# The first MLP with 16 of its 22 up pairs by seven products instead of 15, in another order at the stage's two borders

## The chip, the cores and the metric

One NeuronCore of a Trainium2 chip runs the whole kernel. The metric is the device time of one execution in microseconds (us).

## The reference, cut to what matters

The kernel computes a hybrid layer (gated linear attention and sliding-window attention, then an MLP) followed by two more layers of attention and MLP, for 512 tokens of width 1024 in fp32. The change lies in the MLP of the first layer:

```python
h2 = rms_norm(x, ffn_norm)                                   # 512 x 1024
u = causal_dwconv(h2 @ w_up, conv_w, conv_b)                 # w_up: 1024 x 5632
a, bval = jnp.split(u, 2, axis=-1)                           # 2 x (512 x 2816)
return x + (jax.nn.silu(a) * bval) @ w_down                  # w_down: 2816 x 1024
```

`causal_dwconv` is a depthwise convolution over three tokens. With 128 features to a tile, `w_up` makes 22 pairs of tiles: pair i holds 128 features of `a` and the same 128 of `bval`, and gives f[i] = silu(a) * bval.

## The kernel before

Activations lie with the features on the partitions and the 512 tokens as columns. Every fp32 operand is split into a high part (fp32r, made on ACT by a copy) and a low part (the rest, by a subtraction on POOL or DVE), and each product is taken as high x high + high x low + low x high, summed in a PSUM bank.

**Plain pairs** (`up_tile`, L1217). The first N_PLAIN = 7 pairs are computed tile by tile: 8 blocks of the depth, each with 3 matmuls of 512 columns, so 24 matmuls per tile and 48 per pair. ACT makes the high part of the next weight tile (`split_hi`, L1747), POOL the low part (`split_lo`, L623). DVE scales the bank by rstd (`scaled`, L2828), ACT starts the convolution (`conv_0_of`, L2008), DVE adds its two other taps (`conv`, L2835 and L2838), ACT takes the silu (L2014), and POOL multiplies (`f_made_of`, L726).

**Product pairs** (`up_product`, L1235). The other Q_UP = 15 pairs are computed by a 2 x 2 block scheme of seven products (A11, S1, A12, S2, S4, A22, S3, in this order on PE), each of 4 blocks of depth with 3 matmuls of 256 columns: 84 matmuls of 256 columns per pair. Their left operands are blocks of the raw weights and sums of them (`up_sum` and `up_sum_low` on DVE, `up_copy` and `up_high`, L2042, on ACT, `up_low`, L720, on POOL), held in 14 slots of 512 columns. Their right operands, the seven factors, are made once from x in four parts, inside the plain pairs listed in FACTORS_AT: `factors_first` and `factors_second` on DVE (L2854 to L2865), `factor_highs` on ACT (L2020, L2021), `factor_lows` on DVE (L2871, L2874) and on POOL (L712). No product starts before all four parts have their highs and DVE's lows. The parts with odd number lie in v_tok, which is the same memory as v_split.

Results of the products are put together by ACT copies and DVE additions between them: `p1_copied` (L2047), `p5_copied` (L2054), `u2_copied` (L2060), `u3_copied` (L2066); `c_00`, `c_01`, `c_1`. PE's S2 waits for P1's copy, S4 for P5's, S3 for U2's. P1's copy of the first product pair waits on `scaled` of the last plain tile, because its counter counts all plain tiles first.

**Down projection** (L1291 on). Eight output tiles, each over the 22 f tiles; the weights come as tiles T_DOWN1, T_DOWN1 + 1, ... (T, T+1, ... below), 8 blocks each. For the first output tile (d = 0) PE takes for each weight tile the highs (L1311), then the weight's lows (L1318), and last all lows of f (L1330). f[i] gets its high part on ACT (`f_high`, L2075) and its low part on DVE (`f_low`, L2934); the weights' parts are made by `down_split_hi` (L2084) and `down_split_lo` (POOL, L737). T+2 and T+3 go into memory of the slots, T+2 being needed for f[16] to f[21].

**What sets the order.** Each engine's order is written out by hand, with semaphores between them; an engine that waits holds up all that stands behind it in its queue. SP issues the loads in one queue: raw weight pairs (`up_load`, L572) with odd number go to `stage`, the two buffers that also take all plain weight tiles; those with even number go to other memory. Before the loads of T and T+1 SP waits for

```python
sp.wait_ge(slot_low, UP_LOW_AT[HI_A22, Q_UP - 1 - (Q_UP % 2)])   # L588
```

which is POOL's last reading of the last raw pair in `stage`: pair 13 for Q_UP = 15, pair 15 for Q_UP = 16.

## Time and profile before

| | us |
|---|---|
| median of 3 runs | 1715.41 |
| lowest and highest | 1714.67, 1716.70 |
| the profiled execution's own time | 1717.3 |
| its span, first to last instruction | 1715.0 |
| PE busy | 1697.2 (99%) |
| DVE, POOL, ACT busy | 1136.6, 1027.5, 900.2 |
| mean granted TensorE clock | 0.998 |

The span leaves 2.3 us of the profiled execution's own time outside it. PE's matmuls are pipelined: one of 512 columns is shown 0.39 us long though the next starts 0.23 us after it, so idle time shown for PE is a little less than what the stream of columns loses; start to start is the better measure.

### The profile page before, as it was taken

How to read it: one execution, taken by the hardware profiler on the slowest of the kernel's cores; microseconds unless marked ns; L12 is line 12 of the kernel's file. 1: busy time of each engine (PE TensorE's matmuls, PEld its weight loads, DVE VectorE, ACT ScalarE, POOL GpSimd, SP SyncE). 2: the span in 40 equal slices, each digit the busy share in tenths (PEclk: the TensorE clock that was granted, in tenths of full speed). 3: DMA queues.
4: the chain of work that ended last, by engine and by line, in shares of the span. 5: the costliest groups of instructions: out<-in, count | busy, mean ns of one | idle time of the engine just before them, and what ended most of it. 6: DMA issues, size and time to landing. Idle time of an engine off the chain costs nothing.

```text
span 1715.0 us, 28211 instructions
## 1 busy us (share of the span) xinstructions
PE 1697.2 (99%) x9965; PEld 1458.0 (85%) x9965; DVE 1136.6 (66%) x2214; ACT 900.2 (52%) x1635; POOL 1027.5 (60%) x1076
## 2 busy tenths in 40 slices
PE   9999998999999999999999999999999999999998
PEld 7778887999788778888989898977777889898988
DVE  6875778887511455568757576767677676757576
ACT  5665545787422444435544444546565554545355
POOL 6443688777545434357666666755554665656666
PEclk9999999999999999999999999999999999999999
DMA  5211232232223222223222322232221232222222
GB/s 193 74 68 61 100 124 87 99 111 87 86 99 141 96 68 84 75 81 116 99 101 97 111 96 102 70 129 110 105 102 65 87 135 92 105 99 98 99 98 75
DMA packets 48682, 168.17 MB, mean 98 GB/s; under 512 B 5376, under 2 KB 6672, under 8 KB 48528
## 3 DMA queue, kind: packets, MB, share of 16 engines
q1 hardware_dynamic: 48272, 166.05, 27.6%
q8 instruction: 73, 1.20, 0.3%
q10 hardware_dynamic: 288, 0.52, 0.1%
q14 instruction: 49, 0.40, 0.1%
HBM read 164.31 MB, written 2.24 MB: 97 GB/s over the span
## 4 chain that ended last, share of the span: by engine, by line
PE 80%; DVE 12%; ACT 4%; issue 2%; POOL 1%; DMA 1%; SPq 0%; DVEq 0%; ACTq 0%; POOLq 0%
PE bank L926 18%; PE bank L1685 6%; PE bank L1694 6%; PE bank L1686 6%; PE bank L850 4%; PE bank L851 4%; PE bank L856 4%; PE bank L944 3%; PE bank L950 3%; PE bank L945 3%; PE bank L1266 3%; DVE arena L3438 3%; PE bank L1274 3%; PE bank L1267 3%; PE bank L1318 2%
## 5 line engine op out<-in xcount | busy, mean ns | idle before, releaser
L623 POOL TENSOR_TENSOR w_lo<-stage,w_hi 128x256 fp32r<-128x256 f32 x664 | 532.7, 835 | 421.4 <-ACT w_hi L1747 217.9
L1747 ACT ACTIVATE w_hi<-stage 128x1024 fp32r<-128x1024 f32 x166 | 174.7, 1053 | 156.0 <-PE bank L926 51.7
L851 PE MATMUL bank<-xn_lo,w_hi 128*128 128x512 f32 x544 | 211.7, 389 | 0.0
L850 PE MATMUL bank<-xn_hi,w_hi 128*128 128x512 f32 x544 | 211.7, 389 | 0.0
L926 PE MATMUL bank<-xn_hi,w_hi 128*128 128x512 f32 x464 | 189.0, 407 | 0.0
L926 PE MATMUL bank<-xn_lo,w_hi 128*128 128x512 f32 x464 | 181.8, 392 | 0.0
L3418 DVE TENSOR_TENSOR x<-x,bank 128x256 f32<-128x256 f32 (+1 forms) x217 | 97.5, 455 | 89.2 <-PE bank L1694 86.5
L1694 PE MATMUL bank<-arena 128*128 128x256 f32 x896 | 146.6, 283 | 0.0
L856 PE MATMUL bank<-xn_hi,w_lo 128*128 128x512 f32 x544 | 135.0, 389 | 0.0
L1685 PE MATMUL bank<-arena 128*128 128x256 f32 x512 | 129.4, 284 | 1.3 <-DVE arena L3438 0.6
L1686 PE MATMUL bank<-arena 128*128 128x256 f32 x512 | 128.7, 283 | 0.0
L1694 PEld LDWEIGHTS bank<-arena 128*128 128x128 f32 x896 | 124.8, 192 | 0.0
L926 PE MATMUL bank<-xn_hi,w_lo 128*128 128x512 f32 x464 | 123.9, 398 | 0.0
L856 PEld LDWEIGHTS bank<-xn_hi,w_lo 128*128 128x128 f32 x544 | 102.1, 188 | 21.2
L851 PEld LDWEIGHTS bank<-xn_lo,w_hi 128*128 128x128 f32 x544 | 102.1, 188 | 21.1
L850 PEld LDWEIGHTS bank<-xn_hi,w_hi 128*128 128x128 f32 x544 | 102.2, 188 | 20.9
L3438 DVE TENSOR_TENSOR arena<-tmp,arena 128x256 fp32r<-128x256 f32 (+2 forms) x128 | 115.5, 921 | 3.8 <-ACT arena L2453 2.5
L926 PEld LDWEIGHTS bank<-xn_hi,w_hi 128*128 128x128 f32 x464 | 87.2, 188 | 25.1 <-issue 8.5
L926 PEld LDWEIGHTS bank<-xn_hi,w_lo 128*128 128x128 f32 x464 | 84.6, 188 | 22.8 <-issue 6.0
L926 PEld LDWEIGHTS bank<-xn_lo,w_hi 128*128 128x128 f32 x464 | 87.3, 188 | 16.0
L1685 PEld LDWEIGHTS bank<-arena 128*128 128x128 f32 x512 | 98.2, 192 | 2.8 <-issue 2.7
L1686 PEld LDWEIGHTS bank<-arena 128*128 128x128 f32 x512 | 98.2, 192 | 0.0
(511 smaller groups left out, 4308.9 us busy)
## 6 DMA issues: line engine op xcount, KB each, us to landing
stage<-weights SPq DMA_DIRECT2D x189, 512.0 KB, 3.2
stage<-pairs SPq DMA_DIRECT2D x46, 512.0 KB, 3.2
prob<-pairs SPq DMA_DIRECT2D x32, 512.0 KB, 3.3
bias<-table SPq DMA_DIRECT2D x11, 896.0 KB, 5.5
xn_raw<-pairs SPq DMA_DIRECT2D x14, 512.0 KB, 4.1
out<-y SPq DMA_DIRECT2D x8, 256.0 KB, 2.2
x<-x_in SPq DMA_DIRECT2D x3, 512.0 KB, 7.3
bias<-swa_table SPq DMA_DIRECT2D x4, 256.0 KB, 3.6
```

The source lines that it names most:

```text
L623: ins = nc.gpsimd.tensor_tensor(w_lo[:, p_, ks], stage[:, p_, ks], w_hi[:, p_, ks].bitcast(F32), ALU.subtract)
L850: pe.matmul(G[p_][:], w_hi[:, p_, k], hi[:, k], start=(first and k == ks[0]), stop=False)
L851: mm = pe.matmul(G[p_][:], w_hi[:, p_, k], lo[:, k], start=False, stop=False)
L856: mm = pe.matmul(G[p_][:], w_lo[:, p_, k], hi[:, k], start=False, stop=(last and k == ks[-1]))
L926: mm = pe.matmul(G[p_][:], (w_hi if i < 2 * KD else w_lo)[:, p_, k], (xn_lo if i < 2 * KD and i % 2 else xn_hi)[:, k], start=(i == 0), sto ...
L944: pe.matmul(G[dd][:], w, ff_hi[:, k], start=(k == k0), stop=False)
L1685: pe.matmul(region, w, fc_hi[:, i, f], start=(fresh and i == 0), stop=False, skip_group_check=True)
L1686: pe.matmul(region, w, fc_lo[:, i, f], start=False, stop=False, skip_group_check=True)
L1694: mm = pe.matmul(region, w, fc_hi[:, i, f], start=False, stop=(i == QUADS - 1), skip_group_check=True)
L1747: act.activation(w_hi[:, p_], stage[:, p_], ACT.Copy).then_inc(hi_ready, 1)
L3418: dve.tensor_tensor(dst, dst, src, ALU.add).then_inc(product_added, 1)
L3438: dve.tensor_tensor(fc_lo[:, i, a:b + 1].rearrange("p c s -> p (c s)"), src, fc_hi[:, i, a:b + 1].rearrange("p c s -> p (c s)").bitcast(F3 ...
```

## The change

N_PLAIN goes from 7 to 6, so one pair moves from the plain way to the seven products and Q_UP becomes 16. FACTORS_AT stays at pairs 0, 1, 3, 4, of which 4 is now the last of the loop. The first slots to be filled (A11, S1, A12, S2) move from v_split and bias_slots to bias_slots and rstd_slot, and S4 and S3 to v_split, so that ACT's wait for all factor lows stands ahead of S4's high instead of A11's. The down projection's T+2 and T+3 swap their places, and T+3's high now waits for the last product. In the plain loop ACT makes the factor highs ahead of the next weight's highs; DVE makes the factor lows ahead of the convolution's taps and the second half of the factors ahead of the second convolution. At the end of the products ACT takes f[11] and f[12] ahead of the last U3 copy, f[13] ahead of the last convolution's start, and all of f[16] to f[21] ahead of T+3's high; DVE does `c_1` of the last pair ahead of f_low of f[9].

```diff
--- before.py
+++ after.py
@@ -48,7 +48,7 @@
 
 N_IN = 18
 N_OUT = KD
-N_PLAIN = 7
+N_PLAIN = 6
 FACTORS_AT = [0, 1, 3, 4]
 Q_UP = NF1 - N_PLAIN
 N_UP1 = 2 * N_PLAIN
@@ -223,8 +223,8 @@
         flat_bias = bias[:].rearrange("p a b c -> p (a b c)")
         factor = arena[:, N_IN_ARENA:2 * NF1].rearrange("p (c a r) s -> p c a (r s)", c=7, a=2)
         factor_parts = [arena_raw[:, 6:10].rearrange("p k s -> p (k s)"), v_tok[:].rearrange("p a b t f -> p (a b t f)")]
-        up_slots = ([v_split[:, a, b].rearrange("p t f -> p (t f)") for a in range(2) for b in range(2)] +
-                    [bias_slots[:, k] for k in range(7)] + [rstd_slot[:]])
+        up_slots = [bias_slots[:, k] for k in range(7)] + [rstd_slot[:]]
+        up_slots += [v_split[:, a, b].rearrange("p t f -> p (t f)") for a in range(2) for b in range(2)]
         up_slots += [xn_hi[:, 0], xn_hi[:, 1]]
         up_hi = {k: up_slots[2 * i] for i, k in enumerate(SLOT_ORDER)}
         up_lo = {k: up_slots[2 * i + 1] for i, k in enumerate(SLOT_ORDER)}
@@ -251,18 +251,18 @@
 
         def down_hi(t):
 
+            if t == T_DOWN1 + 3:
+                return v_split[:, 0].rearrange("p b t f -> p (b t) f")
             if t == T_DOWN1 + 2:
-                return v_split[:, 0].rearrange("p b t f -> p (b t) f")
-            if t == T_DOWN1 + 3:
                 return bias_slots[:, 0:2].rearrange("p a (c f) -> p (a c) f", f=P)
             a = N_IN_ARENA + 4 * F_FREE[t % 2]
             return arena[:, a:a + 2].rearrange("p a (c f) -> p (a c) f", f=P)
 
         def down_lo(t):
 
+            if t == T_DOWN1 + 3:
+                return v_split[:, 1].rearrange("p b t f -> p (b t) f")
             if t == T_DOWN1 + 2:
-                return v_split[:, 1].rearrange("p b t f -> p (b t) f")
-            if t == T_DOWN1 + 3:
                 return bias_slots[:, 2:4].rearrange("p a (c f) -> p (a c) f", f=P)
             a = N_IN_ARENA + 4 * F_FREE[t % 2] + 2
             return arena[:, a:a + 2].rearrange("p a (c f) -> p (a c) f", f=P)
@@ -2078,7 +2078,7 @@
 
                 act.wait_ge(stage_full[t % 2], 16 * (t // 2 + 1))
                 if t < T_DOWN1 + 4:
-                    act.wait_ge(product_done, N_PROD * (Q_UP - 1) + (1, 2, UP_AT[HI_S1], UP_AT[HI_S2])[t - T_DOWN1])
+                    act.wait_ge(product_done, N_PROD * (Q_UP - 1) + (1, 2, UP_AT[HI_S1], UP_AT[HI_S3])[t - T_DOWN1])
                 else:
                     act.wait_ge(hi_free, t - 1)
                 act.activation(down_hi(t), stage[:, t % 2], ACT.Copy).then_inc(hi_ready, 1)
@@ -2092,17 +2092,17 @@
                     up_copy(0)
                 silu(i)
                 conv_0_of(i, 1)
+                if i in FACTORS_AT:
+                    factor_highs(FACTORS_AT.index(i))
                 if i < N_PLAIN - 2:
                     split_hi(T_MLP1 // 2 + i + 2, 0)
-                if i in FACTORS_AT:
-                    factor_highs(FACTORS_AT.index(i))
-            act.wait_ge(ff_ready, FF_PREP)
-            act.wait_ge(factor_low, QUADS)
             up_high(HI_A11, 0)
             up_high(HI_S1, 0)
             up_high(HI_A12, 0)
             conv_0_of(N_PLAIN - 1, 0)
             up_high(HI_S2, 0)
+            act.wait_ge(ff_ready, FF_PREP)
+            act.wait_ge(factor_low, QUADS)
             up_high(HI_S4, 0)
             up_copy(1)
             for q in range(Q_UP):
@@ -2140,20 +2140,21 @@
                 conv_0_of(i, 0)
                 if more:
                     up_high(HI_A22, q + 1)
+                else:
+                    f_high(11)
+                    f_high(12)
                 if q + 2 < Q_UP:
                     up_copy(q + 2)
             u3_copied(Q_UP - 1)
-            f_high(11)
-            f_high(12)
+            f_high(13)
             conv_0_of(NF1 - 1, 1)
             silu(NF1 - 1)
-            for f in range(13, 16):
-                f_high(f)
+            f_high(14)
+            f_high(15)
             down_split_hi(T_DOWN1 + 2)
-            for f in range(16, NF1 - 1):
+            for f in range(16, NF1):
                 f_high(f)
             down_split_hi(T_DOWN1 + 3)
-            f_high(NF1 - 1)
             load_exp_and_ln()
             n_split = 4
             for d in range(KD):
@@ -2935,16 +2936,16 @@
 
             for i in range(N_PLAIN - 1):
                 scaled(i, 0)
-                conv(i, 0)
                 if i - 1 in FACTORS_AT:
                     factor_lows(FACTORS_AT.index(i - 1))
+                conv(i, 0)
                 if i in FACTORS_AT:
                     factors_first(FACTORS_AT.index(i))
                 scaled(i, 1)
+                if i in FACTORS_AT:
+                    factors_second(FACTORS_AT.index(i))
                 if i < N_PLAIN - 2:
                     conv(i, 1)
-                if i in FACTORS_AT:
-                    factors_second(FACTORS_AT.index(i))
             if N_PLAIN - 2 in FACTORS_AT:
                 factor_lows(FACTORS_AT.index(N_PLAIN - 2))
             for k in (HI_S1, HI_S3, HI_S2, HI_S4):
@@ -2978,8 +2979,8 @@
                 elif EARLY_AT <= q < EARLY_AT + N_EARLY:
                     f_low(q - EARLY_AT)
                 conv(i, 0)
+            c_1(Q_UP - 1)
             f_low(N_EARLY + 1)
-            c_1(Q_UP - 1)
             f_low(N_EARLY + 2)
             conv(NF1 - 1, 1)
             for f in DVE_LOWS:
```

## Rows read from the trace of the kernel before

**Rows 1.** The page, part 1: busy time, share of the span, instructions.

```profile
PE 1697.2 (99%) x9965; PEld 1458.0 (85%) x9965; DVE 1136.6 (66%) x2214; ACT 900.2 (52%) x1635; POOL 1027.5 (60%) x1076
```

**Rows 2.** PE, timeline, plain pairs: start us, length us, line, shape, count, [idle <-releaser].

```profile
210.27 0.39 PE L1226 MATMUL bank<-xn_hi,w_hi 128*128 128x512 f32 x1
...
221.15 0.39 PE L1226 MATMUL bank<-xn_hi,w_hi 128*128 128x512 f32 x1
...
275.61 2.11 PE L1231 MATMUL bank<-xn_hi,w_lo 128*128 128x512 f32 x8 [0.95 <-POOL w_lo L623]
```

**Rows 3.** PE, timeline, product pairs.

```profile
277.56 0.28 PE L1266 MATMUL bank<-arena,v_split 128*128 128x256 f32 x1
...
282.74 0.35 PE L1266 MATMUL bank<-arena,bias_slots 128*128 128x256 f32 x1 [0.71 <-ACT rstd L2047]
...
285.75 0.36 PE L1266 MATMUL bank<-arena,bias_slots 128*128 128x256 f32 x1 [1.35 <-ACT bank L2054]
...
412.50 0.28 PE L1266 MATMUL bank<-arena,v_split 128*128 128x256 f32 x1
```

**Rows 4.** PE, timeline, first tile of the down projection.

```profile
432.66 0.63 PE L1311 MATMUL bank<-w_hi,arena 128*128 128x512 f32 x2
...
442.83 0.50 PE L1311 MATMUL bank<-arena,v_split 128*128 128x512 f32 x1 [0.97 <-ACT arena L2075]
443.63 2.70 PE L1318 MATMUL bank<-arena,v_split 128*128 128x512 f32 x6 [0.30 <-POOL v_split L737]
...
451.73 0.39 PE L1311 MATMUL bank<-w_hi,v_split 128*128 128x512 f32 x1
```

**Rows 5.** Windows, tail: stretch, its length, busy by engine, PEclk, DMA share, GB/s.

```profile
444.00:446.00 2.00, 2.00 (x6) 1.61 (x5) 2.00 (x5) 0.08 (x1) 0.00 (x0) 0.50 0.58 201
```

**Rows 6.** DVE, timeline, last plain pairs.

```profile
255.41 0.75 DVE L2835 SCALAR_TENSOR_TENSOR tmp<-bank,par,tmp 128x511 f32<-128x511 f32 x1 [1.92 <-ACT tmp L2008]
...
256.87 1.24 DVE L2871 TENSOR_TENSOR arena<-arena_raw,arena 128x256 fp32r<-128x256 f32 x1
...
259.17 1.23 DVE L2854 SCALAR_TENSOR_TENSOR v_tok<-x,par,rstd 128x512 f32<-128x512 f32 x1
...
262.79 0.70 DVE L2828 TENSOR_TENSOR bank<-bank,rstd 128x512 f32<-128x512 f32 x1
...
265.79 0.56 DVE L2864 TENSOR_TENSOR v_tok<-v_tok 128x256 f32<-128x256 f32 x1
...
267.14 0.69 DVE L2828 TENSOR_TENSOR bank<-bank,rstd 128x512 f32<-128x512 f32 x1
...
273.50 0.69 DVE L2828 TENSOR_TENSOR bank<-bank,rstd 128x512 f32<-128x512 f32 x1
...
281.43 0.69 DVE L2828 TENSOR_TENSOR bank<-bank,rstd 128x512 f32<-128x512 f32 x1
```

**Rows 7.** ACT, timeline: last factor highs; last product pair.

```profile
267.58 1.47 ACT L2021 ACTIVATE arena<-v_tok 128x1536 fp32r<-128x1536 f32 x1
...
425.16 1.06 ACT L2084 ACTIVATE arena<-stage 128x1024 fp32r<-128x1024 f32 x1
...
427.20 1.05 ACT L2084 ACTIVATE arena<-stage 128x1024 fp32r<-128x1024 f32 x1
...
429.71 0.37 ACT L2060 ACTIVATE rstd<-bank 128x256 f32<-128x256 f32 x1
```

**Rows 8.** POOL, timeline, around the end of the products.

```profile
426.29 2.84 POOL L737 TENSOR_TENSOR arena<-stage,arena 128x256 fp32r<-128x256 f32 x4 [0.72 <-ACT arena L2084]
...
437.39 1.61 POOL L726 TENSOR_TENSOR xn_raw<-tmp 128x512 f32<-128x512 f32 x1 [3.75 <-DVE tmp L2838]
438.96 4.62 POOL L737 TENSOR_TENSOR v_split<-stage,v_split 128x256 fp32r<-128x256 f32 x4
```

**Rows 9.** SP, timeline of the DMA issues; issue to landing for the first two loads.

```profile
413.60 44.81 SPq L489 DMA_DIRECT2D stage<-weights  x7
...
DMA to landing us min/median/max: 3.2/3.7/4.1
```

## The prediction

> **What bounds the kernel.** The page comes first: PE is busy 99% of the span [rows 1], so a change can only shorten PE's stream or close its gaps. All PE times below are start to start. The second view is PE's timeline through the stage. A plain pair takes 221.15 - 210.27 = 10.88 us, a tile 5.44 [rows 2]. The tiles from 210.27 on are 12, ideally 65.28 us, and the first product starts at 277.56 [rows 3]: 2.0 us are lost, in the last pair, where PE waits for weights (0.95 for POOL's low part) [rows 2]. The two product pairs between 412.50 [rows 3] and 432.66 [rows 4] take 20.16, so 10.08 each. Fifteen of them would take 151.2; from 277.56 to 432.66 are 155.1, so 3.9 us are lost, 2.4 of them at the start of the first pair: S2 starts at 282.74 where 277.56 + 3 x 1.44 = 281.88 was due, and S4 at 285.75 where 284.18 was [rows 3]. The first tile of the down projection has 66 matmuls of 512 columns, 66 x 0.227 = 15.0 us, and takes 432.66 to 451.73, 19.1 [rows 4]: 4.1 lost. In it the matmul of f[21] starts at 442.83 behind ACT's f_high, about 1.7 after its due time of 441.1; the lows of T+2 start at 443.63 behind POOL, another 0.6; and the 28 matmuls from 443.63 take 8.10 in place of 6.35, 1.75 more. The third view says why: the granted clock is 0.50 in 444 to 446 [rows 5], the lower level (1.2 GHz), after some 2 us with hardly a matmul. So the stage loses 10 us at its borders, and the change touches all of them; its arithmetic is small.
>
> **The change, part by part** (times in the clock of the old trace).
>
> *The pair itself.* One plain pair goes, one product pair comes: 10.08 - 10.88 = **-0.80** on PE. The other engines have steady slack beside a product pair: PE is busy without a gap there already.
>
> *The end of the plain pairs.* PE needs 10 tiles from 210.27, so the last ends at 264.67, and A11 may start at 264.8. Before, four parts of factors were done two pairs ahead of the end; now the last is made in the last loop round. On the old timing this would be ruin: DVE starts scaling the second tile of pair 4 at 262.79, 9 us after PE finished it (253.8), and has finished the factors only at 267.14 [rows 6]. But DVE had idled, 1.92 us at a time, for ACT's start of the convolution [rows 6], and the new order puts factor work into these waits. I worked DVE's queue through from pair 0: it catches up with PE in pair 2 and starts pair 4 when its first tile is done, 210.27 + 7 x 5.44 = 248.4. From there: scaling 0.6, lows of part 2 2.30 (256.87 to 259.17), taps 1.46 (255.41 to 256.87), first factors 3.62 (259.17 to 262.79), scaling 0.6, second factors 1.35 (265.79 to 267.14) [rows 6]: 258.4. ACT's highs end 1.9 later (269.05 [rows 7] against 267.14), at 260.3, DVE's last lows 1.15 later, at 261.4. That is 3.4 ahead of A11's start. POOL's lows of the last weight tile no longer stand behind the factor lows, so the 2.0 of stalls go. Products start 264.8 in place of 277.56, with a pair less: 277.56 - 10.88 - 264.8 = **-1.9**.
>
> *The first products.* They stay DVE-bound. From the end of the factor lows (274.10, 0.6 after 273.50) to the scaling of the last tile DVE has 7.33 of work (to 281.43), and S2 starts 1.31 after that [rows 3, 6]. The queue there is unchanged: 261.4 + 7.33 + 1.31 = 270.0 against 264.8 + 4.32 = 269.1 due: a stall of 0.9, as before (0.86). ACT's queue from P1's to P5's copy is unchanged, so S4's 1.57 stays. New slots take only a wait away from ACT that is over by then: 0. The chain from 248.4 to 261.4 is put together from durations taken with POOL at work beside DVE, as it will be; a twelfth of it either way, my estimate, is 1 us, and would be passed on to S2 in full. So **+0.1**, between -0.5 (S2's stall can't be less than none) and +1.0.
>
> *The loads of T and T+1.* Nothing in the diff's lines shows this: Q_UP is now even, the last raw pair (15) lies in `stage`, and SP's wait at L588 is for it. The old loads go out at 413.60, 1.10 after pair 13's start [rows 3, 9]; the new ones the same 1.10 after pair 15's, 423.7 where pair 15's start stands for the old 412.50 + 10.08 = 422.6. The first lands 3.2 later, the second, issued 0.5 after it, 4.1 later [rows 9]: 426.9 and 428.3. ACT took T's high at 425.16 and T+1's at 427.20 [rows 7]; now it stands there with P5's and U2's copies behind it. P5's copy follows T's high (0.95) and ends at 428.3; S4 is due at 432.66 - 3 x 1.44 = 428.34. T+1's high starts at 428.35, so the U2 copy, 2.51 after it (427.20 to 429.71 [rows 7]), at 430.9; S3 is due at 431.2 and the copy takes 0.4. PE loses **+0.15**. Bounds: if the first load lands as late as the second, 4.1, all this is 0.9 later, +1.1; if the wait were hidden, 0.
>
> *The first down tile.* f[21]'s high moves ahead of T+3's (1 us): ACT is done with it at about 441.2, in time; the 1.7 in front of 442.83 goes. What is late next: POOL's lows of T+2, which stand behind f[21]'s product on POOL (437.39) and so behind DVE's last taps [rows 8]. DVE has these one f_low sooner by the new order, but the U2 copy and with it C_01, the taps of (21, 0) and C_1 come 1.1 later by ACT's wait; then f_low of f[9] and f[10]. I get POOL free for the lows at 439.3, in place of 438.96. They took 4.62, though the same four operations took 2.84 at 426.29 [rows 8]. In the first case DVE was at its f_lows; it will be again, so I take 4.62: lows of T+2 from 444.0 in place of 443.63. So the f[21] stall is merely swapped for a longer wait on POOL, **+0.4**, with the 28 matmuls at the lower clock as before. The Trainium skill (GPSIMD Engine Reference, Key points) says that GpSimd shares its SBUF interfaces with VectorE and contends with VectorE instructions that have two SBUF inputs, as an f_low has; by that rule 4.62 holds again, while 2.84 would take 1.8 more off. Rows 8 agree with it.
>
> T+3's lows wait on the 20th f low and are due only 5 us into the second down tile: 0. Later stages see the same tiles in the same buffers: 0.
>
> **Sum**: -0.80 - 1.9 + 0.1 + 0.15 + 0.4 = -2.05. The profiled execution has a span of 1715.0 and 2.3 around it; -2.05 gives 1712.95 and 1715.25. Its own 1717.3 stands 1.9 over the median of the runs, 1715.41, which gives 1713.4. A measurement of this kernel tells 0.2% (3.4 us) from no change, so this is "no change".
>
> **Rivals.**
> 1. *The clock stays up in the tail.* The stretch without a matmul will be 2.7 us in one piece in place of two shorter ones around f[21]'s matmul. For a fall speaks that it is longer; against it, that it is solid and lies elsewhere. If the clock holds, 1.75 more is saved: 1711.6. The Trainium skill (TensorE: Matmul & The Clock Gate, The HAM clock gate) says that the monitor runs freely and the point of a change varies from run to run; by that rule equal gaps need not have equal clocks, and no row here decides. Chance 0.2.
> 2. *The tail closes:* POOL's lows at 2.84: 1.8 less, then also no lower clock: -5.6, 1709.8. Against it [rows 8]. Chance 0.05.
> 3. *The clock falls at the first products* too: 2.4 us idle between 281.88 and 285.75 [rows 3] were followed by products at full speed before, but the place moves by 13 us. Costs up to 1.75: 1715.1. Chance 0.15.
> 4. *Slower: DVE doesn't catch up.* S2 waits on DVE's chain at once, us for us, since the slack of 3.4 lies in A11 only. If DVE reaches the end of the last factors at 267.1 as before and not at 258.4, S2 comes 8.7 later: 1713.4 + 8.7 = 1722.1. It decides against the change from 2.1 us of lateness on, measurably from 5.5. For it: DVE was 9 us behind PE. Against it: its idle time before taps, which the order fills. Chance 0.1.
>
> Forecast 0.5. Faster by over 0.2%: rivals 1 and 2, 0.24 (and a little of them falls short); slower: most of rival 4 with a late load, 0.09; the rest 0.67. **Range**: 1710.5 (rival 1 and the low bounds) to 1716.6 (rival 3, first factors and load at their high bounds); rival 2, rival 4 are left out.
>
> **What would show it.** Right: no wait of PE in the last plain pair, A11 at 264.8 with all factor lows done by 262, S2 at about 270.1 behind P1's copy; ACT's high of T waiting for a DMA, 1.8 later against PE than before; f[21] without a stall, one wait on POOL ahead of T+2's lows, ending 11.4 after PE's first down matmul (before 11.0), and granted clock 0.50 behind it. Wrong: A11 or S1 waiting for factor lows (rival 4), a P5 or U2 stall over 1 us in the last pair (load later), a full clock in the tail (rival 1).

## The result, and the profile after

The changed kernel takes 1718.45 us (median of 20 runs, 1715.54 to 1720.44) against 1716.47 for the kernel before (20 runs): ratio 1.0014, 95% interval 1.0008 to 1.0020. It is slower by 2.0 us, where 2.05 us less was forecast. The profiled execution took 1718.22 us with a span of 1716.4, 1.4 more than before. The first line is page part 1 of the changed kernel, to be held against [rows 1].

```profile
PE 1694.8 (99%) x10001; PEld 1459.0 (85%) x10001; DVE 1140.0 (66%) x2222; ACT 903.8 (53%) x1645; POOL 1025.5 (60%) x1073
```

PE is busy for 2.4 us less and the span is 1.4 longer, so PE waits more. The timeline of PE in the changed kernel shows where: the first product, the waits in the first two pairs and the last one, and the first tile of the down projection.

```profile
264.58 0.28 PE L1266 MATMUL bank<-arena,bias_slots 128*128 128x256 f32 x1
...
267.18 0.75 PE L1274 MATMUL bank<-arena,bias_slots 128*128 128x256 f32 x4 [1.48 <-POOL bias_slots L720]
...
272.18 0.36 PE L1266 MATMUL bank<-arena,bias_slots 128*128 128x256 f32 x1 [1.39 <-ACT rstd L2047]
...
275.20 0.35 PE L1266 MATMUL bank<-arena,v_split 128*128 128x256 f32 x1 [1.35 <-ACT bank L2054]
...
286.18 0.36 PE L1266 MATMUL bank<-arena,v_split 128*128 128x256 f32 x1 [0.64 <-ACT bank L2054]
...
421.60 0.28 PE L1266 MATMUL bank<-arena,bias_slots 128*128 128x256 f32 x1
...
429.11 0.36 PE L1266 MATMUL bank<-arena,v_split 128*128 128x256 f32 x1 [1.59 <-ACT bank L2054]
...
433.50 0.63 PE L1311 MATMUL bank<-w_hi,arena 128*128 128x512 f32 x2
...
445.06 2.48 PE L1318 MATMUL bank<-arena,bias_slots 128*128 128x512 f32 x6 [2.55 <-POOL bias_slots L737]
...
453.11 0.39 PE L1311 MATMUL bank<-w_hi,bias_slots 128*128 128x512 f32 x1
```

Start to start, with [rows 2 to 4] beside it:

| term | predicted | measured | from |
|---|---|---|---|
| the pair itself | -0.80 | -0.80 | 10.08 - 10.88 |
| end of the plain pairs | -1.9 | -2.1 | 264.58 - (277.56 - 10.88); 0.1 of it lies before the stage |
| first products | +0.1 | +2.0 | below |
| late load of T, T+1 | +0.15 | +1.75 | S4 at 429.11; due 421.60 + 4 x 1.44 = 427.36 |
| first down tile | +0.4 | +0.54 | (453.11 - 433.50) - (451.73 - 432.66) |
| sum | -2.05 | +1.4 | span 1716.4 - 1715.0 |

421.60 is the start of the last pair's A11. All products take 433.50 - 264.58 = 168.92 where 16 x 10.08 = 161.28 were due, 7.64 lost; 1.75 of them stand before S4 of the last pair and 5.9 at the start. Before it was 3.9, all at the start. Of the 2.0 more, S4 of the first pair shows 2.4: it comes 10.62 behind A11 (275.20 - 264.58), before 8.19 (285.75 - 277.56 [rows 3]); 0.4 is won back in the second pair.

In the stretches of the trace around the tail's wait (the columns as in [rows 5]) the granted clock is at its lower level (1.2 GHz) behind the gap, as before:

```profile
444.00:446.00 2.00, 0.94 (x3) 0.82 (x4) 2.00 (x3) 0.21 (x1) 1.00 (x1) 0.90 0.00 0
446.00:448.00 2.00, 2.00 (x6) 1.58 (x5) 2.00 (x5) 0.00 (x0) 0.57 (x1) 0.50 0.79 256
```

**The first border.** DVE's timeline in the changed kernel, from the last plain tiles to the last factor lows:

```profile
248.47 0.70 DVE L2829 TENSOR_TENSOR bank<-bank,rstd 128x512 f32<-128x512 f32 x1
249.07 0.42 DVE L2872 TENSOR_TENSOR arena<-arena_raw,arena 128x256 fp32r<-128x256 f32 x1
249.41 0.69 DVE L2875 TENSOR_TENSOR arena<-arena_raw,arena 128x512 fp32r<-128x512 f32 x1
250.74 0.75 DVE L2836 SCALAR_TENSOR_TENSOR tmp<-bank,par,tmp 128x511 f32<-128x511 f32 x1 [0.65 <-ACT tmp L2008]
...
252.19 1.30 DVE L2855 SCALAR_TENSOR_TENSOR v_tok<-x,par,rstd 128x512 f32<-128x512 f32 x1
253.42 1.78 DVE L2857 SCALAR_TENSOR_TENSOR v_tok<-x,par,rstd 128x512 f32<-128x512 f32 x1
255.23 2.50 DVE L2859 TENSOR_TENSOR v_tok<-v_tok 128x256 f32<-128x256 f32 x1
257.66 0.96 DVE L2860 TENSOR_TENSOR v_tok<-v_tok 128x256 f32<-128x256 f32 x1
258.65 0.70 DVE L2829 TENSOR_TENSOR bank<-bank,rstd 128x512 f32<-128x512 f32 x1
...
262.94 0.69 DVE L2875 TENSOR_TENSOR arena<-v_tok,arena 128x512 fp32r<-128x512 f32 x1 [0.95 <-ACT arena L2021]
```

and POOL's in the same time:

```profile
252.91 1.74 POOL L726 TENSOR_TENSOR arena_raw<-tmp 128x512 f32<-128x512 f32 x1
254.61 2.84 POOL L712 TENSOR_TENSOR arena<-arena_raw,arena 128x1024 fp32r<-128x1024 f32 x1
257.42 3.37 POOL L623 TENSOR_TENSOR w_lo<-stage,w_hi 128x256 fp32r<-128x256 f32 x4
262.98 2.91 POOL L712 TENSOR_TENSOR arena<-v_tok,arena 128x1024 fp32r<-128x1024 f32 x1 [2.20 <-ACT arena L2021]
265.85 2.52 POOL L720 TENSOR_TENSOR bias_slots<-arena_raw,bias_slots 128x512 fp32r<-128x512 f32 x2
```

DVE starts pair 4 at 248.47, as worked out (248.4). But its four first factors then take 258.65 - 252.19 = 6.46 us and not 3.62. An operation of 256 columns takes 2.50: it starts in POOL's one instruction of 1024 columns and ends 0.28 behind it (257.73, 257.45). In the kernel before the same four stood beside `split_lo` (L623), in four short instructions.

The other terms of DVE's chain moved too. The lows of part 2 take 1.0 us where the sum had 2.30: in [rows 6] POOL was at work beside them, here it is idle. DVE then waits 0.65 for ACT's start of the convolution, the second factors take 0.4 more than worked out, and the last lows end 0.6 behind ACT's highs and not 1.15. Together that is 2.84 + 0.65 + 0.4 - 1.3 - 0.5 = 2.1. So the last lows end at 263.55 (262.94 and the 0.6 of a step), 2.15 behind the forecast 261.4, and S2 starts at 272.18, 2.18 behind the forecast 270.0. Besides, POOL's factor lows of the last part start when the highs end (262.98) and hold up A11's lows behind them (265.85): the first wait of PE, 1.48, which the prediction did not have. It costs nothing of its own, since S2 waits for DVE's chain anyway.

**The load.** SP's timeline of the issues, then ACT's in the last pair; [rows 9] and [rows 7] answer to them:

```profile
422.69 9.40 SPq L489 DMA_DIRECT2D stage<-weights  x3
```

```profile
427.64 1.06 ACT L2084 ACTIVATE arena<-stage 128x1024 fp32r<-128x1024 f32 x1 [3.34 <-DMA stage<-weights]
428.60 0.37 ACT L2054 ACTIVATE bank<-bank 128x256 f32<-128x256 f32 x1
```

SP issues T's load at 422.69, 1.09 behind the last pair's start (forecast 1.10), and it lands 4.9 later, not 3.2. P5's copy, and with it S4, stands behind ACT's wait.

### The profile page after: what moved, and what is told of

Its sections match the earlier page's. It is cut to its first block, busy times and chain, and to the rows that moved or that the text cites. A ratio compares the mean times of both kernels' runs of the same rounds, so it can differ in the third digit from the quotient of the medians.

```text
span 1716.4 us, 28306 instructions
## 1 busy us (share of the span) xinstructions
PE 1694.8 (99%) x10001; PEld 1459.0 (85%) x10001; DVE 1140.0 (66%) x2222; ACT 903.8 (53%) x1645; POOL 1025.5 (60%) x1073
## 4 chain that ended last, share of the span: by engine, by line
PE 87%; DVE 6%; ACT 2%; issue 2%; POOL 2%; DMA 1%; SPq 0%; DVEq 0%; ACTq 0%; POOLq 0%
PE bank L926 18%; PE bank L1685 6%; PE bank L1694 6%; PE bank L1686 6%; PE bank L851 6%; PE bank L850 6%; PE bank L856 6%; PE bank L944 3%; PE bank L950 3%; PE bank L945 3%; PE bank L1266 2%; PE bank L1274 2%; PE bank L1267 2%; PE bank L1318 2%; PE bank L1311 2%; PE bank L1313 2%
## 5 line engine op out<-in xcount | busy, mean ns | idle before, releaser
L623 POOL TENSOR_TENSOR w_lo<-stage,w_hi 128x256 fp32r<-128x256 f32 x656 | 522.5, 830 | 418.5 <-ACT w_hi L1747 219.3
```

What stands on the lines that cost most here:

```text
L623: ins = nc.gpsimd.tensor_tensor(w_lo[:, p_, ks], stage[:, p_, ks], w_hi[:, p_, ks].bitcast(F32), ALU.subtract)
```

## The experiments

Three groups, each with its own runs of the kernel before. All differences are from the changed kernel unless it says otherwise. For each run the table gives, from PE's timeline of its profile: the start of the first product (A11); what the products lose (start of the first down matmul, less A11, less 10.08 per product pair); the idle time of PE before the last pair's S4, or S3 in pair_only, of that; and the first down tile, start to start. Then the span of that execution and the ratio to before of all runs.

| kernel | pairs plain | A11 | products lose | of it last pair | down tile | span | ratio, 95% |
|---|---|---|---|---|---|---|---|
| before | 7 | 277.56 | 3.9 | 0 | 19.07 | 1715.0 | 1 |
| after | 6 | 264.58 | 7.6 | 1.59 | 19.61 | 1716.4 | 1.0014 (1.0008-1.0020) |
| after_again | 6 | 264.80 | 9.8 | 1.71 | 19.48 | 1718.4 | 1.0022 (1.0013-1.0031) |
| pair_only | 6 | 269.58 | 5.8 | 0.94 | 19.45 | 1719.4 | 1.0024 (1.0015-1.0033) |
| orders_only | 7 | 277.27 | 2.1 | 0 | 16.91 | 1710.8 | 0.9978 (0.9968-0.9988) |
| early_load | 6 | 265.42 | 6.9 | 0 | 16.92 | 1714.5 | 1.0000 (0.9991-1.0009) |
| split_lows | 6 | 264.49 | 7.0 | 0.36 | 18.03 | 1714.1 | 1.0006 (0.9997-1.0016) |
| factors_early | 6 | 270.21 | 5.5 | 1.40 | 18.03 | 1718.4 | 1.0020 (1.0011-1.0029) |
| tail_swap | 6 | 264.80 | 6.9 | 0.33 | 15.44 | 1711.9 | 1.0000 (0.9990-1.0009) |
| all_three | 6 | 269.98 | 2.5 | 0 | 14.99 | 1712.2 | 0.9992 (0.9983-1.0001) |
| pool_order | 6 | 264.85 | 9.2 | 1.72 | 19.63 | 1718.2 | 1.0012 (1.0003-1.0021) |
| best_six | 6 | 264.59 | 7.2 | 0 | 14.99 | 1711.6 | 0.9993 (0.9984-1.0002) |
| seven_tail | 7 | 275.97 | 2.2 | 0 | 14.99 | 1707.6 | 0.9965 (0.9953-0.9977) |

### pair_only: the pair without the orders

```diff
--- before.py
-N_PLAIN = 7
+N_PLAIN = 6
```

> The kernel before with N_PLAIN = 6 and nothing else. Theory A (the new order is what lets DVE finish the factors in time): DVE finishes the last factors several us late, the first products wait for them, S2 comes 5 to 9 us late; the late load of T adds 1 to 2 us; 7 to 10 us slower than before. Rival B (the order in the plain loop hardly matters, the moved pair brings all the cost itself): within 1 us of the changed kernel, so about 1.5 to 2.5 us slower than before.

Measured: 1720.36 us, ratio 1.0024. PE's timeline, the first product:

```profile
269.58 0.58 PE L1266 MATMUL bank<-arena,v_split 128*128 128x256 f32 x1 [4.97 <-ACT v_split L2042]
```

and DVE's, the same four operations as above:

```profile
258.95 1.23 DVE L2854 SCALAR_TENSOR_TENSOR v_tok<-x,par,rstd 128x512 f32<-128x512 f32 x1
...
261.35 0.84 DVE L2858 TENSOR_TENSOR v_tok<-v_tok 128x256 f32<-128x256 f32 x1
262.12 0.41 DVE L2859 TENSOR_TENSOR v_tok<-v_tok 128x256 f32<-128x256 f32 x1
262.57 0.70 DVE L2828 TENSOR_TENSOR bank<-bank,rstd 128x512 f32<-128x512 f32 x1
```

With the old order they take 3.62 us (262.57 - 258.95), but come 6.8 later. So the new order brings DVE forward, and it is this shift against POOL's queue that makes them 6.46. A11 waits 4.97 for the factors and the slots, and the whole is 4.1 us slower than before by the ratio, 5.0 between the medians. That lies between the two expectations (7 to 10, and 1.5 to 2.5): A11 is late as theory A has it, but the products then lose 1.8 less than in the changed kernel (5.8 against 7.6).

### orders_only: the orders without the pair

```diff
-N_PLAIN = 6
+N_PLAIN = 7
```

> The changed kernel with N_PLAIN = 7 again: all the reordering and the moved slots, but 15 product pairs, so the last raw pair is not in stage and L588 waits for pair 13. Theory A: no DMA wait on ACT at T's high, no stall of the last S4, no weight stall in the last plain pair, the down projection's first tile about as long as before (18 to 19.6 us); 1 to 4 us faster than before. Rival B (the orders themselves cost the time): slower than before by about what the change is, 2 us.

Measured: 1711.88 us, 0.9978: a clear gain of 3.8 us (0.0022 x 1715.4). In the table, against before, it is -0.3 for A11, -1.8 in the products and -2.2 in the down tile. Against the changed kernel's span (1716.4 against 1710.8) the pair therefore costs 5.6, and the table gives its parts: -0.8 for the pair, -1.8 for A11 (264.58 against 277.27 - 10.88), +5.5 lost in the products (1.75 of it at the load) and +2.7 in the down tile. The last was not in the prediction: with seven plain pairs the wait for T+2's lows is short and the clock stays up behind it. PE's timeline of orders_only:

```profile
440.99 1.67 PE L1318 MATMUL bank<-arena,bias_slots 128*128 128x512 f32 x6 [1.59 <-POOL bias_slots L737]
...
447.51 0.39 PE L1311 MATMUL bank<-w_hi,bias_slots 128*128 128x512 f32 x1
```

The six lows take 1.67 in place of 2.48, and from there to the next tile are 6.52 in place of 8.05.

One row of DVE in this profile warns against taking short POOL instructions for harmless:

```profile
240.50 4.36 DVE L2855 SCALAR_TENSOR_TENSOR arena_raw<-x,par,rstd 128x512 f32<-128x512 f32 x1
```

It has two inputs in SBUF, and POOL is at work beside it without a pause until 244.31, in instructions of 256 columns (`split_lo`) and one `f_made`. It ends 0.55 behind the last of them. In the changed kernel the same operation beside the same work took 0.99; in early_load it took 4.23 and in split_lows 3.16.

### early_load: the load of T and T+1 off its late place

```diff
-            sp.wait_ge(slot_low, UP_LOW_AT[HI_A22, Q_UP - 1 - (Q_UP % 2)])
-            loads(T_DOWN1, T_QKV[0])
+            sp.wait_ge(slot_low, UP_LOW_AT[HI_A22, Q_UP - 2])
+            for r in range(2):
+                sp.dma_start(down_raw(T_DOWN1 + r), weights[T_DOWN1 + r]).then_inc(stage_full[r], 16)
+            loads(T_DOWN1 + 2, T_QKV[0])
```

`down_raw` is free memory of the raw pairs (xn_raw 8 to 11), which ACT and POOL then read in place of `stage`.

> The changed kernel, with the raw tiles T and T+1 loaded into xn_raw blocks 8 to 11 as soon as pair 14 is read, instead of stage after pair 15. Theory A (the load behind pair 15 is a cost of its own): the last S4's stall of 1.75 us goes, and ACT, DVE and POOL reach the tail earlier, so that the lows of T+2 start 10 to 10.5 us after PE's first down matmul instead of 11.6; 2 to 4 us faster than the changed kernel. Rival B (DVE's chain sets the tail anyway): S4's stall goes and the same time is lost again in the tail, 0 to 0.5 us faster.

Measured: 1716.28 us, 1.0000. ACT's timeline shows T's high without a wait, and PE has no wait in the last pair; the wait in the tail (PE's row) is 1.59 as in orders_only:

```profile
426.12 1.06 ACT L2092 ACTIVATE arena<-xn_raw 128x1024 fp32r<-128x1024 f32 x1
```

```profile
444.01 1.67 PE L1326 MATMUL bank<-arena,bias_slots 128*128 128x512 f32 x6 [1.59 <-POOL bias_slots L745]
```

So the late load costs twice: the stall before S4, and, through POOL, whose lows of T and T+1 come late, 1 us more gap in the tail, behind which the clock fell. In the table that is 1.59 and 2.7 us; of the 2.7, 1.6 is the clock, since split_lows has the long gap (2.55) with the clock up and takes 18.03. Only part of it shows in the span (1.9 less). A11 came 0.8 later in this run, its first border lost 1.0 more (with the operation of 4.23 us DVE ends the last lows 1.6 later), and behind the down tile it took 0.7 longer. By the ratios the gain is 2.4 us, the low end of theory A.

### split_lows: POOL's long instruction cut in four

```diff
-                nc.gpsimd.tensor_tensor(factor[:, F_T1:, 1, ks], factor_parts[k % 2][:, 2 * S:].rearrange("p (c s) -> p c s", c=4),
-                                        factor[:, F_T1:, 0, ks].bitcast(F32), ALU.subtract).then_inc(factor_low, 1)
+                for c in range(4):
+                    ins = nc.gpsimd.tensor_tensor(factor[:, F_T1 + c, 1, ks], factor_parts[k % 2][:, 2 * S + c * HS:2 * S + (c + 1) * HS],
+                                                  factor[:, F_T1 + c, 0, ks].bitcast(F32), ALU.subtract)
+                ins.then_inc(factor_low, 1)
```

> The changed kernel, with POOL's factor lows as four instructions of 256 columns instead of one of 1024. Theory A (a DVE operation with two SBUF inputs is held up for as long as one POOL instruction, so a long one holds it long): DVE's 256-column L2859 beside it falls from 2.50 us to about 1, the first factors from 6.46 to 4 to 4.5, and all behind them comes about 2 us earlier: A11's lows without a stall, S2 1.5 to 2 us earlier, kernel 1.5 to 2 us faster than the changed kernel. Rival B (what is shared is the bandwidth, whatever the length): first factors 6 us or more, no change beyond 0.3 us.

Measured: 1717.39 us, 1.0006. DVE's timeline, then POOL's:

```profile
252.97 1.30 DVE L2857 SCALAR_TENSOR_TENSOR v_tok<-x,par,rstd 128x512 f32<-128x512 f32 x1
254.20 1.77 DVE L2859 SCALAR_TENSOR_TENSOR v_tok<-x,par,rstd 128x512 f32<-128x512 f32 x1
256.01 0.85 DVE L2861 TENSOR_TENSOR v_tok<-v_tok 128x256 f32<-128x256 f32 x1
...
257.77 0.70 DVE L2831 TENSOR_TENSOR bank<-bank,rstd 128x512 f32<-128x512 f32 x1
```

```profile
255.39 3.63 POOL L713 TENSOR_TENSOR arena<-arena_raw,arena 128x256 fp32r<-128x256 f32 x4
```

The one DVE operation falls from 2.50 to 0.85 and the four from 6.46 to 4.80, though POOL's work has become longer (3.63, not 2.84). It is the length of POOL's instruction that DVE was held for. What is left of the excess is 1.77 for 1.22, beside `f_made` (1.74 long). S2 comes only 0.7 earlier (271.50), since the operation of 3.16 us had made DVE 0.8 late at the first factors. The landing of T's load happened to be a quick one here (3.7), and PE lost 0.36 in the last pair. The gain over the changed kernel, 1.1 us between the medians, can't be told from nothing: the intervals of the two ratios overlap. So the cause of DVE's 2.50 is shown in the trace, and not by the time of the whole kernel.

### after_again: the changed kernel once more, beside the next three

> The changed kernel once more, in the same chip job as the next three. Theory A (the load of T behind pair 15 lands at times that differ from execution to execution, and PE waits for all of it above about 3.3 us): time as measured, about 0.1 to 0.2% over before; in this profile the load's time to landing and the last S4's stall move together (stall = landing - 3.2, within 0.3 us), and both differ from the first profile's 4.9 and 1.75. Rival B (4.9 is what this load always takes here, something beside it slows it): landing 4.8 to 5.0 again.

Measured: 1720.17 us, 1.0022. Here the clock fell at the first products as well (rival 3). The windows of this run:

```profile
268.00:272.00 4.00, 3.90 (x24) 3.90 (x25) 3.93 (x7) 1.67 (x3) 3.56 (x4) 0.71 0.00 0
272.00:276.00 4.00, 2.81 (x18) 2.43 (x17) 2.78 (x5) 3.98 (x8) 1.99 (x3) 0.87 0.01 2
```

S4 stands 8.07 behind A11's lows (276.17 - 268.10), as in the first profile (275.20 - 267.18 = 8.02): the slow matmuls lie in what S2's wait would have been. pool_order and best_six show the same: S4 is 8.05 behind A11's lows in both, with the clock up in the one and fallen in the other. The products lose 2.2 us more than in the first profile (9.8 against 7.6). 0.75 of it is in the first pair, and begins with a plain weight tile whose load ACT waited for, 1.14 us where the first profile has 0.27:

```profile
249.94 1.06 ACT L1747 ACTIVATE w_hi<-stage 128x1024 fp32r<-128x1024 f32 x1 [1.14 <-DMA stage<-weights]
```

ACT's start of the convolution stands behind it, so DVE begins its first factors 0.96 later (253.15), and S4 comes 0.97 later. Another 1.3 is in the second pair (S4 to S4 12.29, and 10.98 in the first profile). The lower clock is not needed for that: split_lows shows 12.19 there at the full clock.

T's load landed 5.0 us after its issue, as rival B has it. But split_lows and tail_swap, with the same load, show 3.7, so 4.9 is not what it always takes; and landing less 3.2 gives PE's stall within 0.2 us each time, as theory A has it.

### factors_early: the last part of the factors one pair sooner

```diff
-FACTORS_AT = [0, 1, 3, 4]
+FACTORS_AT = [0, 1, 2, 3]
```

> The changed kernel with FACTORS_AT = [0, 1, 2, 3]: the last factors a pair sooner. Theory A (the first products are late because the last factors are made in the last round, with DVE's first factors stretched to 6.5 us by POOL's work): A11's lows without a stall, S2's stall 0.3 to 1 us in place of 1.55, 2.5 to 3.5 us faster than the changed kernel. Rival B (the first products are bound by the sums and the scaling of the last tile, whatever the factors do): A11's stall goes, but S2 and S4 come as late after the last tile as before: 0 to 1.5 us faster.

Measured: 1719.36 us, 1.0020, no gain. PE's timeline has new waits in the plain pairs:

```profile
242.09 2.10 PE L1231 MATMUL bank<-xn_hi,w_lo 128*128 128x512 f32 x8 [0.73 <-POOL w_lo L623]
...
255.87 2.11 PE L1231 MATMUL bank<-xn_hi,w_lo 128*128 128x512 f32 x8 [1.36 <-POOL w_lo L623]
...
258.92 0.50 PE L1226 MATMUL bank<-xn_hi,w_hi 128*128 128x512 f32 x1 [0.94 <-ACT w_hi L1747]
```

A11's lows and S2 no longer wait, and the products lose 4.3 us less than in after_again (5.5 against 9.8). But A11 starts at 270.21, 5.4 later. Four parts in four pairs in a row are more than ACT and POOL can do beside the weights; the same work, due earlier, takes its price before the border.

### tail_swap: T+2's parts ahead of the last product of f

```diff
@@ POOL
             down_split_lo(T_DOWN1 + 1)
-            f_made_of(NF1 - 1)
             down_split_lo(T_DOWN1 + 2)
+            f_made_of(NF1 - 1)
@@ ACT
             f_high(13)
+            down_split_hi(T_DOWN1 + 2)
             conv_0_of(NF1 - 1, 1)
             silu(NF1 - 1)
             f_high(14)
             f_high(15)
-            down_split_hi(T_DOWN1 + 2)
```

> The changed kernel with T+2's high on ACT ahead of the last convolution's start, and its lows on POOL ahead of f[21]'s product. Theory A (the tail's wait is POOL's queue: f[21]'s product and then lows slowed by DVE): the wait ahead of T+2's lows falls from 2.55 to under 0.5 us, the granted clock stays at its upper level behind it; PE's first down tile takes 15 to 16.5 us in place of 19.6; 3 to 4.5 us faster than the changed kernel. Rival B (f[21]'s high becomes late instead, since its product now stands behind the lows): the wait moves to the last L1311, 1 us or more, 0.5 to 2 us faster.

Measured: 1715.82 us, 1.0000, 4.35 less than after_again in the same group. POOL's timeline:

```profile
435.65 3.63 POOL L737 TENSOR_TENSOR bias_slots<-stage,bias_slots 128x256 fp32r<-128x256 f32 x4
439.23 1.74 POOL L726 TENSOR_TENSOR xn_raw<-tmp 128x512 f32<-128x512 f32 x1
```

The lows are done before PE wants them. In this tile PE waits 0.15 for f[21]'s high and nowhere else, the clock is 1.00 in all windows from 440 to 446, and the tile takes 15.44 us, of which 15.0 is arithmetic.

### all_three: early_load, factors_early and tail_swap

> Early load of T and T+1, factors a pair sooner and the swap in the tail together on the changed kernel. Theory A (three separate places, so the gains add): 7 to 10 us faster than the changed kernel, 1708 to 1711 us, faster than the kernel before by 0.3 to 0.5%. Rival B (one gives back what another saves): 3 to 6 us faster than the changed kernel.

Measured: 1714.67 us, 0.9992. The tail has no wait left (14.99) and the products lose only 2.5, but the waits in the plain pairs are those of factors_early and take it back: A11 at 269.98. At 5.5 us less than after_again it is within rival B's 3 to 6: theory A had added up gains that two of the parts don't have together.

### pool_order: POOL's long instruction moved instead of cut

```diff
                 split_lo(T_MLP1 // 2 + i + 1, 0)
+                if i == 4:
+                    split_lo(T_MLP1 // 2 + i + 1, 1)
                 if i:
                     f_made_of(i - 1)
                 if i - 1 in FACTORS_AT:
                     factor_lows(FACTORS_AT.index(i - 1))
-                split_lo(T_MLP1 // 2 + i + 1, 1)
+                if i != 4:
+                    split_lo(T_MLP1 // 2 + i + 1, 1)
```

> The changed kernel, with POOL's order in the last round of the plain loop changed: both lows of the last weight pair first, then f[3]'s product and the third factor lows, so that DVE's first factors run beside L623 and no longer beside L726 and L712. Theory A (the failing term is DVE's first factors, 6.46 us beside L726 and the long L712 against 3.62 beside L623): L2855 to L2860 take 3.6 to 4.2 us, the last lows end 2 to 2.8 us sooner, A11's lows have no stall or under 0.5 us, S2's stall is near 1 us; 2.5 to 4 us faster than the changed kernel. Rival B (L623 slows DVE as much, its rows of before were lucky): first factors 5.5 us or more, under 1 us faster.

Measured: 1717.55 us, 1.0012, as the changed kernel. DVE's timeline, then POOL's:

```profile
253.17 1.30 DVE L2858 SCALAR_TENSOR_TENSOR v_tok<-x,par,rstd 128x512 f32<-128x512 f32 x1
...
257.42 0.70 DVE L2832 TENSOR_TENSOR bank<-bank,rstd 128x512 f32<-128x512 f32 x1
258.02 1.50 DVE L2868 TENSOR_TENSOR v_tok<-v_tok 128x256 f32<-128x256 f32 x1
259.55 2.50 DVE L2869 TENSOR_TENSOR v_tok<-v_tok 128x256 f32<-128x256 f32 x1
```

```profile
257.95 1.29 POOL L726 TENSOR_TENSOR arena_raw<-tmp 128x512 f32<-128x512 f32 x1
259.20 2.57 POOL L712 TENSOR_TENSOR arena<-arena_raw,arena 128x1024 fp32r<-128x1024 f32 x1
```

The first factors fall to 4.25 (257.42 - 253.17), as they should if what POOL does beside them makes them slow. But now the second factors lie beside POOL's two long instructions, the first 1.50 and the second again 2.50, where they took 0.93 and 0.85. Each ends 0.28 behind the POOL instruction that it started in (259.52 and 259.24, 262.05 and 261.77). The cause is confirmed a second time, and the gain is nil: the contention has been moved along DVE's chain, not taken out. The last lows even end 1.0 later than in the changed kernel (264.51), because ACT waited 1.00 us for a plain weight tile's load and DVE began its first factors that much later (253.17).

### best_six: pool_order, early_load and tail_swap

> The changed kernel with POOL's new order, the early load of T and T+1 and the swap in the tail. Theory A (three separate places): 7 to 10 us faster than the changed kernel, 1709 to 1712 us, spans within 1 us of each other in nearly all runs, since no load and no fall of the clock is left that differs. Rival B (one gives back what another saves, as with the factors a pair sooner): 1713 us or more.

Measured: 1714.12 us, 0.9993. The load and the tail cost nothing any more (14.99); the first border still loses 7.2, and the clock fell in it (granted 0.62 from 268 to 272). The contention that pool_order only moves is still there, so the border's share of what was expected did not come, and the time is rival B's (1713 us or more).

### seven_tail: seven plain pairs, the new orders and tail_swap

> The changed kernel with N_PLAIN = 7 and the swap in the tail: 15 product pairs, all orders new. Theory A: the tail's wait of 1.59 us goes; 1 to 2 us faster than orders_only, near 1710 us, and 0 to 2 us faster or slower than best_six, since the pair itself is worth only 0.8 us. Rival B (the tail is already closed enough): within 0.5 us of orders_only.

Measured: 1709.6 us (6 runs, 1708.24 to 1711.37), 0.9965 (0.9953 to 0.9977). It beats both kernels, the one before by about 6 us. PE does not wait in the last plain pairs, the products lose 2.2 and the tail nothing. Against tail_swap the only difference is the pair: it costs 4.3 us by the spans (1711.9 against 1707.6) and about 6 by the ratios (1.0000 against 0.9965).

## Why the prediction was wrong

**The pair, -0.80:** right, as a term of PE's stream. What the runs add is that the pair is worth no more than that, and that with it the kernel is 4 to 7.5 us slower in every comparison (pair_only 4.1 over before, after and after_again 6.2 and 7.5 over orders_only, tail_swap 6 over seven_tail, by the ratios): it has to have its factors a pair sooner, and its number being odd or even decides when T is loaded.

**The end of the plain pairs, -1.9:** right. A11 at 264.58 (forecast 264.8), no wait in the last plain pair, DVE at pair 4 at 248.47 (248.4). Rival 4 (DVE doesn't catch up) did not occur as it was told. But its price did, for a part: "S2 waits on DVE's chain at once, us for us" held with 2.18 us.

**The first products, +0.1, was 2.0: the step that failed.** It was the term "first factors 3.62", taken from [rows 6] with the sentence that the durations were "taken with POOL at work beside DVE, as it will be". POOL was at work in both, but with another instruction: four of 256 columns before, one of 1024 and one `f_made` of 512 after. I had worked DVE's queue through the new order and left POOL's where it was. split_lows (4.80) and pool_order (4.25) show this cause. The first factors alone were 2.84 too short. The same sentence had put the lows of part 2 at 2.30, and there it erred the other way: without POOL beside them they took 1.0. With the other terms above, the chain came 2.15 late; the twelfth of 13 us that I allowed was 1 us. The rows held the sign of it already: in [rows 6] an operation of 256 columns (L2871) took 1.24 and another 0.56, and in [rows 8] an f_low of DVE beside POOL made four of POOL's operations 4.62 in place of 2.84, which I used in the tail and for POOL alone. The Trainium skill (GPSIMD Engine Reference, Key points) names contention with VectorE instructions that have two SBUF inputs, and these have. The trace agrees. What it cost DVE here, 2.50 for 0.41 to 0.85, the rows above show.

**The load, +0.15, was 1.75.** The mechanism was right in every step: SP's wait on pair 15, ACT standing before P5's copy, S4. The size was off. I took 3.2 for the landing of the first load, what it was in the one profile of before [rows 9]; it was 4.9 and 5.0 in the two profiles of the changed kernel, which cost 1.59 and 1.71 of idle time, and 3.7 in split_lows and tail_swap, which cost 0.36 and 0.33. The other kernels with this load show 3.2 (pair_only, where the second load took 5.2 and PE waited 0.94 before S3), 4.7 (factors_early) and 5.1 (pool_order). My upper bound of 4.1 was the second load's in that same profile, and too low.

**The first down tile, +0.4, was 0.54.** Right in time and in all its parts: f[21] in time, one wait on POOL, its lows 4.59 long, ending 11.56 behind the first matmul (11.4), the lower clock behind it. What was not seen is that this wait hangs on the load: by early_load and orders_only it is 1.59 without the late load, and then the clock stays up. So the same term, with the pair left where it was, would have been -2.2 (16.91 - 19.07).

**The rivals.** Rival 1 (clock up in the tail) came in two profiles of six-pair kernels with the old tail and the late load, split_lows and factors_early; rival 3 (clock falls at the first products) in after_again. Neither decided the sign. What would have is a rival in which the order that DVE catches up by puts it beside POOL's long instructions. Together the two missed sizes are 1.9 + 1.6 = 3.5 us, the whole distance between the forecast span, 1712.95, and 1716.4.

**Open:** why, with the same code there, the second pair took between 10.98 and 12.29 us from S4 to S4, and why the DVE operation at 240.5 was held for 4.36 us in one profile and not in the next. Both are part of why the first border lost between 6 and 8 us.

## What to carry to other kernels

When an engine's queue is moved by some microseconds, its durations have to be read again beside what the other engines will be doing then: a DVE operation with two SBUF inputs that starts in a POOL instruction ended only behind it here, so a long POOL instruction can hold it long. Short ones mostly let it in between, but not always (4.36 us in orders_only). Before a unit of work is moved for its own 0.8 us, test the orders and the move apart: here the orders alone gave 3.8 us, the move took 4 to 7.5, and one more swap of the queue that held the tail gave 2.2 more. And a load that sits in front of an engine's queue is priced at its slow landing, not its quick one.

## What the runs showed of the hardware

- A DVE operation of 256 columns with both inputs in SBUF took 0.41 to 0.43 us with POOL idle, mostly 0.84 to 0.96 beside POOL's instructions of 256 columns, and 2.50 in one of 1024 columns (2.84 and 2.57 long, in the changed kernel and in pool_order). With that instruction cut in four of 256 columns it took 0.85.
- What it takes in a long POOL instruction is the rest of that instruction and 0.28: ends of 257.73 and 257.45 in the changed kernel, 262.05 and 261.77 in pool_order. Before, an operation (L2871) that started late in such an instruction took only 1.24 (ends 258.11 and 257.82).
- A DVE operation of 512 columns with one input in PSUM was not held: L2890 took 0.68 in POOL's instruction of 2.91 (262.98 to 265.89, changed kernel), as in other places.
- Short POOL instructions back to back held a DVE operation of 512 columns for 4.36, 4.23 and 3.16 us in orders_only, early_load and split_lows, until 0.55 behind the last of them; in the changed kernel it took 0.99 at the same place.
- T's load, 512 KB and the first of two, landed 3.2 us after its issue before, 3.7 in split_lows and tail_swap, and 4.9 and 5.0 in the two profiles of the changed kernel; over all kernels here that load it into `stage`, 3.2 to 5.1.
- Equal gaps of PE gave different clocks. Behind gaps of 2.53 to 2.55 us in the tail it fell to the lower level in after, after_again and pool_order, and not in split_lows and factors_early; from there to the next tile took 8.05 us in after and 6.48 in factors_early (454.98 - 448.50). At the first products, behind a wait of 2.12 or 2.13 for A11's lows, it fell in after_again and best_six and not in early_load and pool_order; behind 1.59 in the tail (orders_only, early_load) it stayed up both times. By the Trainium skill (TensorE: Matmul & The Clock Gate, The HAM clock gate) the point of a change varies from run to run; these runs agree, in that equal gaps did not give equal clocks. At the first products the fall cost nothing that shows: S4 was 8.05 behind A11's lows with it (best_six) and without it (pool_order).
